# A two-layer diffusion step on one core: the first projection is cut in two halves of its contraction, later modulation chunks move between attention units, and a table assigns ring slots

## The reference

```python
m = silu(cond) @ w_mod[l] + b_mod[l]              # (6 * 1024) per group: shift, scale, gate, shift, scale, gate
h = x * (1 + scale1) + shift1
# layer 0: z = h @ w_in_ab (1024 x 1184) -> query latent 256, key/value latent 128, rotary key 32,
#          8 query heads of 64, 2 key heads, 2 value heads
#   q_a = rms_norm(latent) @ w_uq ; k, v from ckv @ w_ukv ; 8 latent heads + 8 grouped heads with a sink
# layer 1: z = h @ w_in_c (1024 x 1536), 16 query and 4 key/value heads
x = layer_norm(ALPHA * x + gate1 * (attention(...) @ w_out))
h = x * (1 + scale2) + shift2
x = layer_norm(ALPHA * x + gate2 * moe(h))        # 16 experts, top 1 group of 4, top 2 experts in it
```

## Time and profile before

| | |
|---|---|
| median of three runs | 883.5 us (882.17 to 884.71) |
| the profiled execution | 889.22 us, span 887.4 us |
| TensorE matmuls busy | 777.7 us, 88% of the span |
| DVE / ACT / GpSimd busy | 299.0 / 147.7 / 63.4 us |
| traffic | 287.34 MB, mean 324 GB/s |
| chain that ended last | PE 54%, DMA 21%, DVE 15%, SP queue 4% |

### The profile page before, as it was taken

How to read it: one execution, slowest core, us unless ns; L and a number is a source line. 1 busy time by engine, 2 the same in 40 slices (tenths; PEclk the granted TensorE clock), 3 DMA queues, 4 the chain that set the end, 5 groups by cost and what they waited for, 6 DMA issues and landing times.

```text
span 887.4 us, 9784 instructions
## 1 busy us (share of the span) xinstructions
PE 777.7 (88%) x3715; PEld 378.6 (43%) x3715; DVE 299.0 (34%) x595; ACT 147.7 (17%) x386; POOL 63.4 (7%) x126
## 2 busy tenths in 40 slices
PE   4799888989999998979988988997799999889694
PEld 1345544545443443324334635545544443433231
DVE  0003444463421212211454064537422221122066
ACT  0201232222110111101112112322211110111020
POOL 0000000001100011001000030000200001101000
PEclk9599699997999998999999996997799999989997
DMA  8999920189999999999999699322089999999951
GB/s 310 370 325 401 388 101 27 69 321 399 422 428 418 419 427 424 422 422 423 408 376 329 219 389 419 129 96 95 0 343 419 429 418 419 430 422 413 428 207 48
DMA packets 68795, 287.34 MB, mean 324 GB/s; under 512 B 4972, under 2 KB 10604, under 8 KB 60564
## 3 DMA queue, kind: packets, MB, share of 16 engines
q1 hardware_dynamic: 64724, 275.59, 77.7%
q10 hardware_dynamic: 2880, 7.03, 2.0%
q0 software_dynamic: 1152, 4.19, 1.2%
HBM read 278.99 MB, written 7.82 MB: 323 GB/s over the span
## 4 chain that ended last, share of the span: by engine, by line
PE 54%; DMA 21%; DVE 15%; SPq 4%; issue 3%; ACT 2%; POOL 1%; DVEq 0%; ACTq 0%; POOLq 0%
DMA ring<-in_exp_w_up 19%; PE bank L991 16%; PE bank L735 9%; PE bank L1019 7%; PE bank L824 6%; PE bank L772 3%; SPq L575 3%; PE bank L669 3%; DMA ring<-in_w_mod 2%; DVE arena L1511 2%; PE bank L959 2%; PE bank L803 2%; PE bank L781 2%; PE bank L648 1%; ACT arena L1625 1%
## 5 line engine op out<-in xcount | busy, mean ns | idle before, releaser
L991 PE MATMUL bank<-ring,arena 128*64 128x512 f32 x1024 | 236.3, 618 | 25.3 <-DMA ring<-in_exp_w_up 24.5
L991 PEld LDWEIGHTS bank<-ring,arena 128*64 128x64 f32 x1024 | 80.5, 142 | 177.6 <-issue 177.6
L1019 PE MATMUL bank<-ring,arena 128*64 128x512 f32 x512 | 113.4, 595 | 4.6 <-DMA ring<-in_exp_w_down 3.6
L1509 DVE TENSOR_SCALAR arena<-arena 128x256 f32<-128x256 f32 x32 | 9.4, 294 | 250.6 <-ACT arena L1664 250.3
L735 PE MATMUL bank<-ring,arena 128*128 128x512 f32 (+2 forms) x224 | 76.2, 503 | 0.7 <-ACT arena L1598 0.7
L1588 ACT ACTIVATE arena<-bank 128x512 f32<-128x512 f32 (+6 forms) x79 | 40.9, 538 | 160.9 <-PE bank L735 68.0
L959 PE MATMUL bank<-arena 128*128 128x128 f32 x512 | 64.4, 281 | 3.0 <-POOL arena L1815 3.0
L1019 PEld LDWEIGHTS bank<-ring,arena 128*64 128x64 f32 x512 | 36.3, 137 | 69.9 <-issue 67.0
L959 PEld LDWEIGHTS bank<-arena 128*128 128x128 f32 x512 | 61.6, 198 | 4.0 <-POOL arena L1815 3.1
L669 PE MATMUL bank<-ring,cwin 128*32 128x512 f32 x384 | 50.9, 683 | 11.6 <-DMA ring<-in_w_mod 11.6
L824 PE MATMUL bank<-ring,arena 128*128 128x512 f32 x128 | 61.0, 611 | 0.0
(11 more groups left out here) (166 smaller groups left out, 632.9 us busy)
## 6 DMA issues: line engine op xcount, KB each, us to landing
ring<-in_exp_w_gate SPq DMA_DIRECT2D x32, 2048.0 KB, 26.5
ring<-in_exp_w_up SPq DMA_DIRECT2D x32, 2048.0 KB, 24.2
ring<-in_exp_w_down SPq DMA_DIRECT2D x32, 2048.0 KB, 29.8
ring<-in_w_mod SPq DMA_DIRECT2D x24, 2048.0 KB, 19.0
expert_rows<-arena ACTq DMA_DIRECT2D x12, 512.0 KB, 9.2
ring<-in_w_out_ab SPq DMA_DIRECT2D x2, 2048.0 KB, 19.6
ring<-in_w_in_c SPq DMA_DIRECT2D x2, 2048.0 KB, 24.9
ring<-in_w_out_c SPq DMA_DIRECT2D x2, 2048.0 KB, 10.5
```

Source lines behind the costliest of these rows:

```text
L991: mm = nc.tensor.matmul(pb(key)[SLOTS * hf:SLOTS * (hf + 1), :], xeT[b][:, k * P + SLOTS * a:k * P + SLOTS * (a + 1)], w[:, :, k, hf * 256 ...
L1019: mm = nc.tensor.matmul(pb(key)[SLOTS * a:SLOTS * (a + 1), :], hp[:, c:c + SLOTS], block_ap(n + a)[:, kf * D + hf * HALF:kf * D + (hf + 1) ...
```

## The change

**Loads.** The start now loads chunk 0 and chunk 2 (half of the first shift, half of the first scale), `x` behind them, then one block with contraction rows 0 to 511 of the first 928 columns of `w_in_ab`; then chunks 1 and 3 and the block with rows 512 to 1023; then the last 256 columns whole. After it: `lora`, `w_out_ab` half 1, chunks 4 to 9, half 0, chunks 10 and 11, layer 1's chunks 0 to 3. Both orders have 22 blocks and the same bytes. A table `EVEN_SLOTS` names the slot of each of the 22, the experts keep n % 9, and `plan_slots` counts the uses of each slot.

**Start of layer 0** (`begin_even`). Every step of the start is split by contraction half h: `first_ab(h)` on DVE, `first_turned(h)` on ACT, `input_turned(g, h)` and `even_part(b, g, h)` on TensorE. The half-0 matmuls of the first two column pieces stay open in banks 4 to 7 while chunks 1 and 3 are multiplied.

**Latents first.** `normalise_even` no longer waits for the whole z: it normalises the latents when piece 0 is there, rotates the query heads later and the key heads last. The transposes of the grouped heads are split by group: group 1's stand behind the second unit's scores (step `g1`).

**Modulation pairs.** `modulation(0, 1)`, `modulation(0, 2)` and `modulation(1, 0)` are gone. Six steps `mc` take their place, one behind the steps of each of the units 1 to 6, with two chunks each; all use bank 7, and DVE adds (or for layer 1's first pair copies) the bank into `mods`. `mod_columns(0, 1)` moves ahead of the last Y, as layer 1 had it.

```diff
+MOD_HALVES = ((0, 2), (1, 3))
+MOD_PAIRS = [(0, 4), (0, 6), (0, 8), (0, 10), (1, 0), (1, 2)]
...
+    for h in range(2):
+        order += [("mod", 0, c) for c in MOD_HALVES[h]] + [("win", 0, h)]
+    order += [("win", 0, 2), ("lora", 0, 0), ("wout", 0, 1)] + [("mod", 0, c) for c in range(4, 10)]
+    order += [("wout", 0, 0)] + [("mod", 0, c) for c in (10, 11)] + [("mod", 1, c) for c in range(4)]
...
+EVEN_SLOTS = {("mod", 0, 0): 0, ("mod", 0, 2): 4, ("win", 0, 0): 5, ("mod", 0, 1): 6, ("mod", 0, 3): 7,
...
@@ attention_steps
+    if layer == 0:
+        steps.append(("g1", 0))
...
             steps += make.get(u, [])
+            if 1 <= u <= len(MOD_PAIRS):
+                steps.append(("mc", u - 1))
...
@@ plan_turns
+                    elif name == "mc":
+                        t.use(step, 7)
...
@@ TensorE
+            def mod_pair(key):
+
+                l, c = MOD_PAIRS[key[1]]
+                room(pe, key)
+                mod_chunk(pb(key), l, c, True)
+                mod_chunk(pb(key), l, c + 1, False)
+                mod_end(key, l, (l, c) == (1, 0))
...
+            def begin_even():
+
+                key = ("mod0", 0)
+                room(pe, key)
+                mod_chunk(pb(key), 0, 0, True)
+                mod_chunk(pb(key), 0, 2, False)
+                mod_end(key, 0, True)
+                for g in range(G):
+                    input_turned(g, 0)
+                pe.wait_ge(*saved(key))
+                turn_rows(("modT", 0, 0, 0), mods[0], C_SEL, 8)
+
+                key = ("mod0", 1)
+                even_part(0, 0, 0)
+                even_part(0, 1, 0)
+                room(pe, key)
+                mod_chunk(pb(key), 0, 1, True)
+                even_part(1, 0, 0)
+                mod_chunk(pb(key), 0, 3, False)
+                mod_end(key, 0, False)
+                even_part(1, 1, 0)
+                pe.wait_ge(*saved(key))
+                turn_rows(("modT", 0, 0, 1), mods[0], C_SEL, 8)
+                input_turned(0, 1)
+                even_part(2, 0, 0)
+                even_part(2, 1, 0)
+                input_turned(1, 1)
+
+                for b in range(2):
+                    for g in range(G):
+                        even_part(b, g, 1)
+                zz = z[0]
+                pe.wait_ge(s_cache, 64)
+                pe.wait_ge(s_zfin, 1)
+                transposes(("qlatT",), [zz[:, g, c * P:(c + 1) * P] for g in range(G) for c in range(2)])
...
+                for g in range(G):
+                    even_part(2, g, 1)
...
@@ DVE, attention
+                    elif name == "g1":
+                        dve.wait_ge(*full(("kT", 0, 1)))
+                        V.tensor_copy(kbT[:, P:3 * P], pb(("kT", 0, 1))[:, 0:2 * P]).then_inc(*drain(("kT", 0, 1)))
+                    elif name == "mc":
+                        m = mods[MOD_PAIRS[u][0]][:]
+                        dve.wait_ge(*full(step))
+                        if MOD_PAIRS[u] == (1, 0):
+                            V.tensor_copy(m, pb(step)[:]).then_inc(*drain(step))
+                        else:
+                            if u > 0:
+                                dve.wait_ge(*saved(("mc", u - 1)))
+                            V.tensor_tensor(m, m, pb(step)[:], ALU.add).then_inc(*drain(step))
...
@@ TensorE, ln_rows, route
-                if (l, s) == (0, 0):
-                    modulation(0, 2, (lora_n, index[("wout", 0, 0)]))
...
-                if l == 0:
-                    modulation(1, 0)
```

334 lines of the change are left out of this document (209 added, 125 removed).

## The result

Over six runs of each the changed kernel took 891.2 us in the median (888.8 to 895.3) and the kernel before 885.1: a ratio of 1.0077, 95% interval 1.0039 to 1.0115. A second set of twelve runs gave 1.0062 (1.0034 to 1.0090). It is slower by some 6 us, where 3.4 less were forecast.

A forecast was written before the change was run, and what follows sets the result against it. Waits for modulation chunks bound the start, nearly full TensorE the attention, DMA the experts. 20.0 - 26.2 + 7.0 + 2.6 = 3.4 us less: 885.8 traced, 880.1 on the median; own range 876 to 884, with rivals 872 to 888.5.

The forecast's parts named there:

- I take 6 us at the low level ... 3 us lost: Split start, from first projection: TensorE at low clock for 6 us, costing 3 us, bounds 1.9 and 9.2.
- 39.5 of work: Split start: 39.5 us of TensorE work from first projection matmul at 26.7 to the last transpose before the scores.
- Rival A: Split start: clock stays low, 8.3 us more in all, 888.4 us; decided by a low stretch past 13 us; chance 0.20.
- It lay 5.7 above the median of the three runs, and on the median the same 3.4 give 880.1: Whole kernel: the profiled 889.2 lay 5.7 above the median; 3.4 less gives 885.8 traced, 880.1 on the median.
- ACT's copies out of bank 7: Pairs of units 1, 3 and 5 wait for ACT to free bank 7: 9.8 plus 7.3 of 26.2 us lost.
- the tail of layer 1: Gates to first expert: layer 0 without modulation there matches layer 1's 41.61 against 49.18; 7.0 us gained.
- the full ring: Experts: weight ring full at the first expert, last gate weights 198.15 us behind it, not 200.77; 2.6 us gained.
- Second turn: Second unit's turn at 84.3, not 104.34: 13.6 us after first scores at 70.7; 20.0 us gained.
- x "lands by about 21": Start: x is loaded behind two chunks and not four, so it lands by about 21 us.
- B: Pairs between units: cheap if ACT's copies leave bank 7 in time, costing 18.7, 7.5 more gained, 872.6 us; chance 0.15.
- C: Pairs between units: DVE's additions lie on the path, ahead of the turn's copy; 4.1 us lost, 884.2 us; chance 0.15.
- D: Experts: the full ring frees them from the DMA, some 25 us gained in place of 2.6, about 858 us; chance 0.04.

The follow-up runs named there:

- x behind the half block: Changed kernel with the two loads of x issued behind the first half block, not ahead of it; 890.8 us, ratio 1.0075 to the kernel before.
- filled start: Changed kernel plus matmuls nobody reads, three between chunks 0 and 2, two before unit 1's pair; 887.7 us, ratio 1.0034 to the kernel before.
- w_out behind: Split start, chunk pairs around first scores and first turn, first w_out block loaded behind chunks 4 to 7; 871.9 us, with three filling matmuls 871.4.
- pairs first: Changed kernel with the chunk pairs of units 1, 3 and 5 ahead of their unit's other steps; 883.6 us, ratio 0.9989 to the kernel before.
- second trace of the changed kernel: The changed kernel run again without edits, twelve runs; median 891.0 us, ratio 1.0062 to the kernel before, the traced execution 885.4 us.
- split start alone: Changed kernel with modulation pairs undone: chunks 4 to 7 ahead of the heads' transposes, the rest placed as before the change; 888.1 us, ratio 1.0035.
- pairs first with filling: Changed kernel with units 1, 3 and 5's pairs ahead of other steps and three unread matmuls between chunks 0 and 2; 880.7 us, ratio 0.9954.

## Why the prediction was wrong

The measured 891.2 is 11.1 above the forecast of 880.1. The forecast had two parts, a sum for a traced execution (885.8) and a step from there to the median (5.7 less). Both failed. The trace at the median of its runs, that of x behind the half block, is 4.9 above the sum, and the step down of 5.7 was not there for the changed kernel: together 10.6 of the 11.1.

*"I take 6 us at the low level ... 3 us lost".* This was the mis-sized term, the cost of the low clock. In the first trace of the changed kernel the closing matmul, the transposes and the columns took 5.3 us and not the 2.9 that the prediction had "at the high clock". From the first projection matmul to the last transpose in front of the scores it took 41.8, 2.3 over the 39.5 of work, where 3.0 were allowed. And 4.7 went in the pairs of units 1, 3 and 5, where the prediction asked only for the idle time. Together that is 9.5 and not 3.0; in the second trace it is 1.6, in the one at the median some 5.5. The rest of the late start is no clock: chunk 2 was used from 20.52 and not 18.29, 2.2 us, and in the other unfilled traces with x in its place it was used from 18.40 to 20.19.

The prediction's price for chunk 2, 3.48 us from the earlier trace rows, was itself that of slow matmuls (1.92 where the start is filled), so it set a chunk at the low clock in front of steps "at the high clock". So the 26.71 of the filled start agrees with the forecast 26.7 by two errors that cancel, a chunk 1.6 us later and 1.6 us quicker.

How often the matmuls behind a wait run at the low clock differs from wait to wait. These are all traces in which the wait stands unfilled:

| wait in front of | idle us | traces | matmuls behind it slow |
|---|---|---|---|
| chunk 2 | 2.53 to 4.80 | 8 | 7 |
| pair of unit 1 | 1.99 to 2.00 | 4 | 1 |
| pair of unit 3 | 1.99 to 2.00 | 5 | 1 |
| pair of unit 5 | 2.55 to 2.56 | 5 | 5 |

Of the seven slow ones at chunk 2, three show the clock rise by 14.7 to 15.4 us and fall at 18.1 to 18.9, in the wait (both traces of the changed kernel and w_out behind). In the other four it was not lost there but not yet gained: the clock's first rise on record comes at 34.3 to 35.2 us in three and at 23.8 in one, behind the start of chunk 2. In the trace of pairs first it rose at 16.5 and stayed until 26.7.

The single slow cases of units 1 and 3 are from one trace, the first of the changed kernel, whose 895.3 us are the longest of its 18 runs. Where the waits were taken away (pairs first, without and with filling), all pairs took 3.64 or 3.65.

The first projection matmul stands at 25.48 to 31.50 in the eight traces whose start is not filled, four of them at 30.9 or later; the four filled ones lie at 26.1 to 26.7. Why the clock is lost in the same wait, or comes late, in one execution and not in another stays open.

The two edits that remove these losses gained 6 to 8 us (pairs first, some 1.5 of it clock and the rest wait in the second trace) and another 3 (filling), and with both the kernel is ahead of the one before by 4. The edit to the pairs pays more than their clock costs, because it also takes out the waits, which the prediction had priced.

Rival A had the right cause and said 888.4; it placed it behind the start of the projection and had nothing in the pairs. Its condition, a low stretch of more than 13 us, was met in the first trace (from 18.7 to 35.7 us) and not in the second (from 18.9 to 22.3). Of its rule in the Trainium skill, "TensorE: Matmul & The Clock Gate", section "HAM oscillation — how this bites in real kernels", that the clock drops at each wait for weights: three traces agree at the wait for chunk 2 (4.80 us, 0.50 at its end, in the first), and that of pairs first does not, where the wait was 2.53 and chunk 2 took 1.92. They go further as well, since the wait of 2.55 us for a copy, in front of unit 5's pair, dropped it each time.

*"It lay 5.7 above the median of the three runs, and on the median the same 3.4 give 880.1".* This is the second step that failed. The traced execution of before was at the long end of its spread, with a low clock. The changed kernel has such losses in most of its executions: the 885.8 of the sum was reached by one of its three quickest in twelve, not by one 5.7 above its median. The two sets of runs say the medians differ by 5.5 to 7 the other way.

What was right, and what was luck. By the second trace of the changed kernel the forecast looks nearly exact: first projection 27.64 (26.7), second turn 83.72 (84.3), first expert 222.50 (222.1), time 885.4 (885.8). The terms against the first trace of before are 20.6 gained (20.0), 27.8 lost (26.2), 7.5 gained (7.0), 3.5 gained (2.6). The mechanisms were right: ACT's copies out of bank 7, no wait for DVE's additions, the tail of layer 1, the full ring. But the second turn is right by luck: the first scores stand at 68.49, 2.2 before the forecast 70.7, and the chain behind them took 1.6 longer than the 13.6 forecast. And the execution itself was a lucky one, with the clock back early at the start and kept in two of three pairs.

The smaller points. *Second turn*: the 13.6 us from the first scores took 15.0 to 15.2 in every trace of this order, full clock or low at the first scores; the waits in it, of 2.88 and 1.04 us in the second trace, are for DVE. *x "lands by about 21"*: it was waited for nowhere, except where it was moved. *Rivals*: B fell (the waits for bank 7 are all there), C fell (no wait in front of a turn behind a pair), D fell (the last gate weights come 198.08 us behind the first expert, 198.15 forecast).

Whether the change can be called bad as a whole is answered by the last kernels. By the ratios the split start alone costs 3 us, and putting all six pairs between the units costs 2.5 to 4 more. In the second trace the pairs cost 27.7 there against the layout with the pairs undone, and gave back 10.4 ahead of the first scores (7.5 of matmuls, 2.9 of a wait), 8.1 from gates to first expert and 5.9 behind it. The split start pays together with two pairs in the waits around the first scores and the loads ordered for them: that gained most, 12.5 us against the kernel before. Whether these two edits would gain as much with the old start was not tried.

## What to carry to other kernels

Ask of each wait of TensorE not only how long it is but what the clock does behind it: here waits of 2 us halved the speed of the next 3 us in some executions and not in others, and one of 2.55 us did so in each. Before subtracting, find where in its own spread the traced execution lies; two traces of the changed kernel lay 10 us apart here. And move work into waits that stay whatever you do: the 1 to 3 us in front of the first scores and of the first turn took in matmuls that between the units cost nearly their full time.

## What the hardware showed

- The same program gave spans of 883.5 and 893.5 us with waits in front of the pairs that agree to 0.01 us; the difference lies in the stretches at half clock (to 22 or to 36 at the start, one or three pairs) and in when chunk 2 landed (19.49 or 20.52).
- A clock that was kept is not kept for good. In two of the four filled starts it fell one wait later, the one of 2.1 to 2.5 us in front of the projection; in the two others it stayed at full speed there (first piece 5.85 and 5.83 us). Windows of pairs first with filling, one of those where it fell:

```profile
24.00:26.00 2.00, 0.00 (x0) 0.00 (x0) 1.54 (x6) 1.50 (x4) 0.00 (x0) 1.00 1.04 399
26.00:28.00 2.00, 1.71 (x3) 0.84 (x4) 0.00 (x0) 0.00 (x0) 0.00 (x0) 0.72 1.06 392
28.00:30.00 2.00, 2.00 (x4) 1.00 (x3) 0.00 (x0) 0.00 (x0) 0.00 (x0) 0.50 1.05 385
```

- The windows read 1.00 at the start of every trace, but the matmuls there run at the low level. Chunk 0 takes 3.21 to 3.64 us in every trace, where chunk 2 needs 1.92 at full clock. With x behind the half block the windows read 1.00 from 18 to 34 us while chunk 2 takes 3.64 and the closing matmul 1.91. The clock record of each packed trace begins only with its first rise, and the matmuls change speed at that very time: 21.5 us in the kernel before, where the second chunk took 3.48, and 15.9 in its second trace, where it took 1.93. So in these traces a 1.00 ahead of the first rise says nothing; the duration of a known matmul does.
- 5 of a pair's 16 matmuls took 1.91 us, the 8 of a single chunk 1.93, all 16 took 3.64.
